# Modulation products with the weight blocks as the stationary operand

## The reference, cut to what matters

```python
def _modulation(cvec, w, b, n):
    return jnp.split(jax.nn.silu(cvec) @ w + b, n, axis=-1)
# per layer: w is 1024 x 6144, b is 6144; six vectors of 1024 come out for each conditioning vector
h = _rmsnorm(x, norm1_w[l]) * (1.0 + sc1) + sh1        # c's scale and shift
hc = _rmsnorm(cx, norm1_w[l]) * (1.0 + csc1) + csh1    # c_ctx's
x = x + g1 * y                                         # gated residual; the same again with sc2, sh2, g2
```

## Time and profile before

| what | value |
|---|---|
| median of 3 runs (lowest, highest) | 3336.56 us (3333.86, 3338.16) |
| span of the profiled execution | 3326.9 us |
| own time of the profiled execution | not given apart from its span; the median of the runs is 9.7 us above the span |
| TensorE busy, weight loads busy | 3099.7 us (93%), 2660.7 us (80%) |
| VectorE, ScalarE, GpSimd busy | 1220.7, 956.9, 1129.1 us |
| mean granted TensorE clock | 0.968 of full speed |

### The profile page before, as it was taken

The page is one execution under the profiler, slowest core; times in us unless marked ns, Lnnn a source line. Parts: engine busy times, 40 slices in busy tenths (PEclk is TensorE's granted clock), DMA queues, the critical chain, the costliest instruction groups (busy, mean ns, idle before and its releaser), DMA issues. The chain is left out here.

```text
span 3326.9 us, 47831 instructions
## 1 busy us (share of the span) xinstructions
PE 3099.7 (93%) x19520; PEld 2660.7 (80%) x19520; DVE 1220.7 (37%) x2792; ACT 956.9 (29%) x1600; POOL 1129.1 (34%) x614
## 2 busy tenths in 40 slices
PE   6899999999999999999999779899999999989996
PEld 3788887898888997888888657787898778968885
DVE  2344415523333023333333534433532231154455
ACT  2222224432223112222222232222542222233332
POOL 2122240053333433333333232332143335345453
PEclk8999999999999999999999879999999999989998
DMA  5011120012221115211111211111022222222222
GB/s 192 26 52 52 46 88 26 7 53 91 80 83 67 64 58 186 75 64 64 71 64 57 99 55 52 70 58 70 20 80 89 89 89 91 101 95 98 98 89 95
DMA packets 39671, 249.80 MB, mean 75 GB/s; under 512 B 4512, under 2 KB 4896, under 8 KB 14112
## 3 DMA queue, kind: packets, MB, share of 16 engines
q1 hardware_dynamic: 36576, 236.25, 19.8%
q10 hardware_dynamic: 2880, 10.49, 0.8%
HBM read 236.23 MB, written 10.49 MB: 74 GB/s over the span
## 5 line engine op out<-in xcount | busy, mean ns | idle before, releaser
L1868 POOL TENSOR_TENSOR w_rest<-raw,w_head 128x2048 fp32r<-128x2048 f32 (+2 forms) x172 | 740.7, 4307 | 1099.0 <-ACT w_head L1042 1067.0
L687 PE MATMUL psum_products<-w_head,h_head 128*128 128x256 f32 x2368 | 691.4, 292 | 0.0
L687 PE MATMUL psum_products<-w_rest,h_head 128*128 128x256 f32 x2368 | 678.6, 287 | 0.0
L687 PE MATMUL psum_products<-w_head,h_rest 128*128 128x256 f32 x2368 | 677.9, 286 | 0.0
L687 PE MATMUL psum_products<-h_head,w_head 128*128 128x512 f32 (+3 forms) x1696 | 599.8, 354 | 19.4 <-POOL h_rest L1894 17.1
L687 PE MATMUL psum_products<-h_head,w_rest 128*128 128x512 f32 (+3 forms) x1696 | 598.1, 353 | 0.0
L687 PE MATMUL psum_products<-h_rest,w_head 128*128 128x512 f32 (+3 forms) x1696 | 596.9, 352 | 0.0
L687 PEld LDWEIGHTS psum_products<-w_head,h_head 128*128 128x128 f32 x2368 | 462.9, 195 | 2.6 <-issue 1.2
L687 PEld LDWEIGHTS psum_products<-w_rest,h_head 128*128 128x128 f32 x2368 | 463.5, 196 | 0.5
L687 PEld LDWEIGHTS psum_products<-w_head,h_rest 128*128 128x128 f32 x2368 | 462.8, 195 | 0.0
L1042 ACT ACTIVATE w_head<-raw 128x2048 fp32r<-128x2048 f32 (+2 forms) x172 | 307.6, 1789 | 472.7 <-PE psum_products L687 427.9
(11 more groups left out here) (236 smaller groups left out, 4135.9 us busy)
## 6 DMA issues: line engine op xcount, KB each, us to landing
raw<-in_stream SPq DMA_DIRECT2D x198, 1024.0 KB, 4.7
raw<-in_stream SPq DMA_DIRECT2D x20, 512.0 KB, 3.3
residual<-stage ACTq DMA_DIRECT2D x16, 512.0 KB, 2.7
stage<-residual SPq DMA_DIRECT2D x14, 512.0 KB, 4.7
stage<-in_x SPq DMA_DIRECT2D x8, 512.0 KB, 5.9
stage<-in_ctx SPq DMA_DIRECT2D x4, 512.0 KB, 8.2
out<-stage ACTq DMA_DIRECT2D x4, 512.0 KB, 2.6
rope_r<-in_rope_r SPq DMA_DIRECT2D x2, 768.0 KB, 4.2
```

Source lines behind the costliest of these rows:

```text
L687: return nc.tensor.matmul(o, a, b, start=start, stop=stop)
L1868: G.tensor_tensor(wl[:, s["sp"] % 2, 0:n], raw[:, s["n"] % 2, 0:n], wh[:, s["sp"] % 2, 0:n].bitcast(F32), ALU.subtract).then_inc(*ev.mark( ...
```

## The change

The weight block is now the stationary operand and the two vectors the moving one: `lhsT = w[:, k, ct*128:(ct+1)*128]` (128 x 128), `rhs = cvec[:, 2, k, :]` (128 x 2), accumulated over eight k-tiles for each of the two column tiles. The result stands on the partitions at once, where the turn had put it. The copy to `vrow`, the turn and the fifth piece are gone; a piece is now half of one column tile, four matmuls. The numbers of filler pieces handed to `ticks` follow (5 per slot become 4; 11 become 8 in `rtiles`), which shifts pieces between ticks.

```diff
     def vectors(count):
-        turn = None
         for l, n in islice(modulation, count):
             s = cols("mod_w", l, n * COLS, splits=False)
             for piece in range(4):
                 yield step("vector", s, l=l, n=n, piece=piece)
-                if piece == 0 and turn:
-                    yield step("vector", **turn)
-            turn = dict(slot=s, l=l, n=n, piece=4)
-        yield step("vector", **turn)
...
-            pieces = 4 * len(pairs(ctx)) + 1
+            pieces = 4 * len(pairs(ctx))
...
-            ticks("rtiles", len(tiles) + 4, fill, 11, l=l, hd=hd, tiles=tiles)
+            ticks("rtiles", len(tiles) + 4, fill, 8, l=l, hd=hd, tiles=tiles)
...
-        ticks("norms", len(tiles) + 2, fill, 5 * 2 * D // COLS, l=l, use="mid", tiles=tiles, gen=gen)
+        ticks("norms", len(tiles) + 2, fill, 4 * 2 * D // COLS, l=l, use="mid", tiles=tiles, gen=gen)
...
-                    if piece < 4:
-                        for k in (2 * piece, 2 * piece + 1):
-                            last = mm(bank[0:2, 0:COLS], cvec[:, 2, k, :], w[:, k, :], k == 0, k == KD - 1)
-                        last.then_inc(*ev.mark("pe", "vrow", l, st["n"]))
-                    else:
-                        pe.wait_ge(*ev.at("vrow_sb", l, st["n"]))
-                        if (l, st["n"]) == (0, 0):
-                            pe.wait_ge(*ev.at("const"))
-                        for ct in range(2):
-                            last = mm(bank[:, 2 * ct:2 * ct + 2], vrow[0:2, ct * P:(ct + 1) * P],
-                                      c("ident")[0:2, 0:2])
-                        last.then_inc(*ev.mark("pe", "bank", st["bank"]))
+                    ct = piece // 2
+                    for k in range(4 * (piece % 2), 4 * (piece % 2) + 4):
+                        last = mm(bank[:, 2 * ct:2 * ct + 2], w[:, k, ct * P:(ct + 1) * P], cvec[:, 2, k, :],
+                                  k == 0, k == KD - 1)
+                    last.then_inc(*(ev.mark("pe", "bank", st["bank"]) if piece == 3 else ev.mark("pe", "piece")))
...
                 if kind == "vector" and st["piece"] == 3:
-                    dve.wait_ge(*ev.at("vrow", l, st["n"]))
-                    V.tensor_copy(vrow[0:2, :], psg[0:2, st["bank"] % RING, 0:COLS]).then_inc(
-                        *ev.mark("dve", "vrow_sb", l, st["n"]))
-                if kind == "vector" and st["piece"] == 4:
                     n = st["bank"]
                     dve.wait_ge(*ev.at("bank", n))
```

More of the change, by code:

```diff
@@ L426, in backbone @@
         cvec = sb("cvec", [P, 3, KD, 2])
-        vrow = sb("vrow", [P, COLS])
         vec = sb("vec", [P, DEPTH, 6 * KD, 2])
@@ L1014, in _ @@
                 if s is not None:
-                    if kind == "vector" and st["piece"] == 4:
-                        continue
                     ev.now[("w_free", s["n"])] = {"pe": ev.count["pe"]}
```

## The result

| kernel | median (lowest, highest) | span of the profile |
|---|---|---|
| before, same chip, 9 runs | 3333.86 us (3329.01, 3338.16) | 3326.9 us |
| after, 9 runs | 3345.43 us (3338.39, 3353.3) | 3345.6 us |

What follows compares the result with a forecast made beforehand. TensorE, 93% busy, and its clock were taken to bound the kernel. Terms +14.7, +17.1, +2, +51 and +9 summed to +94 us: 3421 us span, 3430.6 as timed; own range 3375 to 3500, with rivals 3315 to 3500.

Steps and rivals of the forecast that it cites:

- 1, start: Products at the start: clock low throughout, loads 0.213 us apart, 54.5 us against 39.8, +14.7 us.
- 2, second norm: Layer 0's second norm: clock low, 61.5 us against 44.4, +17.1; first dense matmuls after it start low, +2.
- 3, price of a fall per 3.4 us: Dense work: a 3.4 us stretch at the low clock costs 1.4 us.
- 4, retention, falls: Eight retention heads: four low stretches of 3.4 us a head in layer 0, six in layer 1, +56 us.
- 4, retention, saving: Retention heads: pieces at the high clock save half of 24 x 0.4 us, -5 us.
- 5, mLSTM: Eight mLSTM heads with one slot: one clock fall a head, 11 us, less 8 x 0.3 saved, +9 us.
- step 4: Retention, 8 heads with 12 pieces each: clock falls +56 us, saving -5, together +51.
- Rival B: Clock falls only at the start and second norm, mixers' own streams hold it: +22, 3358 us; chance 0.20.
- C: Nothing to be seen: low-clock loads keep 0.111 us, or DMA and VectorE set the pace; 3337 us, chance 0.06.
- The premise: TensorE's clock: streamed columns keep it high, loads do little; with only loads and two-column streams, low throughout.
- A: Whole kernel: loads count as work, the clock holds, every place gains; 3318.6 us, chance 0.20.
- the load's 0.213 us at the low level: Weight loads of 128 columns: 0.213 us apart at the low clock, against 0.111 at the high level.

Runs made afterwards that it cites:

- F1: The changed kernel with the two vectors repeated to 64 moving columns everywhere; 3310.99 us, ratio 0.9929 to the kernel before.
- E1: The changed kernel with the two vectors repeated to 128 moving columns, same weight loads; 3288.28 us, ratio 0.9863 to the kernel before.
- E4: The kernel before with the products' stationary operand padded to 128 columns, turns and waits kept; 3319.43 us, ratio 0.9958 to the kernel before.
- E2: Only the mixers' products in the changed form, start and layer 0's second norm as before; 3294.89 us, ratio 0.9883 to the kernel before.
- F2: The changed kernel with the two vectors repeated to 32 moving columns everywhere; 3330.72 us, ratio 0.9988 to the kernel before.

## Why the prediction was wrong

Its steps, with the measured term beside the forecast:

| step | forecast | measured | why |
|---|---|---|---|
| 1, start | +14.7 | +16.0 | right: no rise at all, 0.214 apart |
| 2, second norm | +19.1 | +22.4 | right: low for 64.9 us; 3 us more than forecast |
| 3, price of a fall per 3.4 us | 1.4 | 1.3 and 1.5 | right |
| 4, retention, falls | +56 | +22 | 16 stretches more than F1, where I had 40 |
| 4, retention, saving | -5 | -32 | F1's: 1.32 a slot, not 0.4 |
| 5, mLSTM | +9 | -8.9 | same saving; -7.0 and -2.7 in F1, so nothing paid for falls in layer 0; layer 1 is between -1.9 and -6.5 in the kernels with changed mixers, too wide to tell |
| the rest | 0 | -1.5 | |

**What failed is step 4**, "4 x 4 x 1.4 + 4 x 6 x 1.4 = 56. The pieces at the high level save half of 24 x 0.4: -5. +51." It was -9.5, which is 60 of the 75 us between the sum (+94) and the spans (+18.7). Step 5 is another 18.

The two parts of it come from F1, whose heads cost the same but for the clock and hardly fall (10.2 us of low clock, before 3.4). Its retention is -13.8 and -18.0, together -31.8 for 24 slots: 1.32 us a slot. After is 10.3 us worse than F1 in layer 0 with 27.2 us more of low clock, and 12.0 worse in layer 1 with 27.3 more. That is 0.38 and 0.44 us for each low microsecond, 1.3 and 1.5 us for 3.4: the price of step 3. After's 64.7 us of low clock there are 19 of the forecast's stretches of 3.4 us, where I had said 40; before has one.

**The saving.** "That is 0.4 us less than before" compared 4.37 with 3.95 us a slot. The pitch was right: from a piece's first load to the first load of the group behind it are (986.60 - 985.71)/8 = 0.111 us for each, as in the turns. Two things were missed. The wait of 0.1 us at each piece, taken from the turns, is not there: a piece is 8 x 0.111 = 0.89 us of loads, of which 0.81 pass before the next group starts and the rest in that group (`r_qk`: 0.30 us, 0.23 behind E1's piece). Four are 3.6 us, not 3.95. And before has a cost outside of the rows that I read: up to five times a slot the group *ahead* of a product piece or a turn is 0.09 us longer, as 983.33 - 983.02 = 0.31 against 0.22 shows. Taken in both kernels from the start of the group ahead to the start of the group behind, the saving is at most 4 x 0.15 + 0.53 + 5 x 0.09 = 1.6 us, of which 1.32 arrive. E4 shows the switches at the pieces by themselves: padded to one width, the old form, with its turn, gains 14.6 us in the heads. The row for it stands in the same view as the earlier trace rows, one line above the piece.

**The falls.** "I take the low part as four stretches ... and six" was a guess: its only ground is one pair of stretches. It had the last ticks of a head fall, but there the clock stayed at 0.98. The chain of `r_f`, `r_b` and `r_v` between the pieces, 256 columns each, may be what holds it. This is a reading of the rows; I tried no kernel that takes those streams away. Rival B, in which "the mixers' own streams hold it", with 3358 us, was nearer than my forecast in its time, though not in its letter: the clock does fall in the heads, for 64.7 us. C, with 3337 us, was the nearest in time, by luck alone: it had the loads keep 0.111 us at the low level, and they take 0.213.

**What held.** The premise, "I conclude that loads do little for the clock": 256 loads back to back, 55 us without a gap, left the clock low; with 128 moving columns behind the same loads it rose (E1). Nor is it the busy share that the profile gives: from 6.2 to 46.2 us the changed kernel's TensorE reads busy for 39.78 of 40.00 us and before's for 35.85, and it is before's clock that rose. A, which had loads count as work, is refuted by the same row. The Trainium skill (TensorE: Matmul & The Clock Gate, Part 1, "What's actually happening") lets the clock follow how busy TensorE has been; the trace does not bear that out if a load is taken to be busy time. Also held: the load's 0.213 us at the low level, where the Trainium skill (TensorE: Matmul & The Clock Gate, "LDWEIGHTS") has only columns/1.2 GHz, 107 ns for 128, which the 0.111 us here bears out at the high level alone.

**What stays open.** Why a head falls where it does. After and E2 have the same instructions in the heads and 64.7 against 40.8 us of low clock, so it depends on more than the heads' own code, and after's runs spread over 15 us, before's over 9. With two moving columns the kernel's time is partly a matter of how the heads lie in time. Nor do the runs tell what in a head's first ticks makes it fall; pieces 1.2 us apart stand there (after, from 973 us), but I tried no other placement.

## What to carry to other kernels

A product with few moving columns isn't cheap on TensorE: its load of 128 columns sets the pace, and where nothing else streams the clock stayed at half here, so that all work beside it cost double. Repeat the moving columns (here 64 between other work, 128 where the products stand alone): beside such loads they cost next to nothing, and they held the clock. Take a piece's cost from the start of the group ahead of it to where the groups behind it have their usual length again, for a change of the stationary operand's size is paid in the neighbour.

## What the runs showed of the hardware

- Plain float32 loads of 128 x 128 start 0.11 us apart at the high level with 2, 64 and 128 moving columns (heads of after, F1 and E1: 1.11, 1.11 and 1.12 us for the ten loads from a piece to `r_v`), and 0.213 us apart at the low level with 2, 32, 64 and 128 (the starts of after, F2, F1 and E1).
- Loads with two moving columns left the clock low for 55 us at the start (after), and so did 32 and 64 (F2, F1); with 128 it rose within two slots (E1). In the norm, which begins with the clock high, it was low for 64.9, 61.4, 20.5 and 0 us with 2, 32, 64 and 128.
- A switch between loads of 128 columns and loads of two costs 0.10 us in the group ahead and 0.07 at the change back (before against E4); the load then starts with its piece and not 0.11 us ahead of it. Padding the load to 128 columns takes it away: 15.7 us of the kernel. Ahead of a turn, whose load has 128 columns and two rows, the cost stays (0.32 us in E4, 0.31 before).
- A low stretch in the retention heads costs 0.38 and 0.44 us for each microsecond of it (after against F1, layers 0 and 1).
